# A layer of attention and experts on one core: first scores ahead of the last input projection, lists turned ahead of context products

## The reference

```python
def attn_projections(h, w_in, g_qa, g_ka):       # one projection, split into q, k, v of two head groups
    ...
    qa = rms_norm(heads(qa), g_qa)
    ka = rms_norm(heads(ka), g_ka)
    return qa, ka, heads(va), heads(qb), heads(kb), heads(vb)
...
def latent_layer(...):
    sh1, sc1, gt1, sh2, sc2, gt2 = modulation(c[:, None, :], w_ada, b_ada)
    h = modulate(x, g_pre_attn, sh1, sc1)
    qa, ka, va, qb, kb, vb = attn_projections(h, w_in, g_qa, g_ka)
    qa, ka = rope_2d(qa, rows, cols), rope_2d(ka, rows, cols)
    qb, kb = rope_2d(qb, rows, cols), rope_2d(kb, rows, cols)
    oa = blocked_gqa(qa, jnp.concatenate([k_a_ctx, ka], axis=1), jnp.concatenate([v_a_ctx, va], axis=1))
    ob = windowed_gqa_with_ctx(qb, kb, vb, k_b_ctx, v_b_ctx, sink_b)
    o = jnp.einsum('btk,kd->btd', jnp.concatenate([oa, ob], axis=-1), w_out)
    x = x + gt1 * rms_norm(o, g_post_attn)
    return ffn_sublayer(x, sh2, sc2, gt2, ...)
...
def expert_choice_moe(h, w_router, w_gate, w_up, w_down):
    cap = CAPACITY_FACTOR * T // N_EXPERTS       # 64 latent rows or 16 context rows for each of 16 experts
    aff = jax.nn.softmax(logits, axis=-1)
    g, idx = lax.top_k(jnp.swapaxes(aff, 1, 2), cap)
    xg = jax.vmap(lambda hb, ib: hb[ib])(h, idx)
    a = jnp.einsum('becd,edf->becf', xg, w_gate)
    u = jnp.einsum('becd,edf->becf', xg, w_up)
    y = jnp.einsum('becf,efd->becd', jax.nn.silu(a) * u, w_down) * g[..., None]
    # rows are added back at their tokens
```

## Time and profile before

| what | us |
|---|---|
| median of 3 runs | 955.2 (954.45 to 956.45) |
| the profiled execution | 957.28 |
| its span on the engines | 955.5 |
| PE busy in it | 899.5 (94%) |
| DVE busy | 361.2 (38%) |
| ACT busy | 216.5 (23%) |

### The profile page before, as it was taken

How to read it: one execution, slowest core, us unless ns; L and a number is a source line. 1 busy time by engine, 2 the same in 40 slices (tenths; PEclk the granted TensorE clock), 3 DMA queues, 4 the chain that set the end, 5 groups by cost and what they waited for, 6 DMA issues and landing times.

```text
span 955.5 us, 19886 instructions
## 1 busy us (share of the span) xinstructions
PE 899.5 (94%) x8653; PEld 444.0 (46%) x8653; DVE 361.2 (38%) x953; ACT 216.5 (23%) x526; POOL 89.2 (9%) x124
## 2 busy tenths in 40 slices
PE   3999998899899999779999999999999999999996
PEld 3544444777656565533344443444344334433442
DVE  4255635787767765811112031111111120310126
ACT  3132223676644653410000000000000000000002
POOL 2021200000000000100110111011101100110111
PEclk9999998899999999789999999999999999999998
DMA  9996532300000006959999999999999999999973
GB/s 337 347 373 264 221 132 99 116 2 1 2 1 23 23 23 226 414 185 371 398 395 412 398 398 398 409 397 397 408 399 398 396 410 399 397 400 392 340 277 139
DMA packets 76629, 265.58 MB, mean 278 GB/s; under 512 B 6032, under 2 KB 9808, under 8 KB 76544
## 3 DMA queue, kind: packets, MB, share of 16 engines
q1 hardware_dynamic: 71088, 248.53, 66.3%
q0 software_dynamic: 3792, 12.78, 4.8%
q10 hardware_dynamic: 1664, 3.01, 0.8%
HBM read 251.27 MB, written 13.04 MB: 277 GB/s over the span
## 4 chain that ended last, share of the span: by engine, by line
PE 70%; DMA 14%; SPq 5%; DVE 4%; ACT 3%; issue 2%; POOL 1%; ACTq 0%; POOLq 0%; DVEq 0%
PE ps L927 25%; PE ps L939 12%; DMA ring<-in_w_down 8%; PE ps L635 7%; PE ps L790 6%; SPq L467 5%; PE ps L611 4%; PE ps L741 3%; PE ps L719 3%; PE ps L706 2%; DMA reg_qt<-in_w_gate 2%; DMA ring<-in_w_ada 2%; PE ps L561 2%; ACT ring L1277 1%; DMA reg<-rows_l,kt 1%
## 5 line engine op out<-in xcount | busy, mean ns | idle before, releaser
L927 PE MATMUL ps<-ring,reg 128*32 128x512 f32 x1792 | 201.8, 592 | 0.0
L1809 DVE TENSOR_SCALAR mod<-ps,kt 64x512 f32<-64x512 f32 x30 | 22.5, 750 | 258.7 <-PE ps L927 258.5
L927 PEld LDWEIGHTS ps<-ring,reg 128*32 128x32 f32 x1792 | 58.1, 110 | 112.4 <-issue 103.8
L1329 ACT ACTIVATE reg<-ps 128x256 f32<-128x256 f32 x16 | 6.1, 384 | 386.3 <-PE ps L990 375.4
L939 PE MATMUL ps<-ring,values_in 128*32 128x256 f32 x1536 | 91.5, 380 | 1.5 <-DMA ring<-in_w_up 1.1
L927 PE MATMUL ps<-ring,kt 128*32 128x512 f32 x768 | 86.8, 592 | 0.0
L790 PE MATMUL ps<-ring,reg 128*128 128x512 f32 x160 | 76.4, 604 | 0.0
L939 PEld LDWEIGHTS ps<-ring,values_in 128*32 128x32 f32 x1536 | 48.7, 110 | 50.9 <-issue 16.4
L635 PE MATMUL ps<-ring,reg_qt 128*128 128x512 f32 x160 | 70.6, 594 | 0.0
L939 PE MATMUL ps<-ring,reg 128*32 128x256 f32 x1024 | 62.9, 388 | 3.0 <-DMA ring<-in_w_down 2.2
L1277 ACT ACTIVATE ring<-ps 128x640 f32<-128x640 f32 (+3 forms) x80 | 44.4, 555 | 73.3 <-PE ps L719 70.6
(11 more groups left out here) (224 smaller groups left out, 1001.2 us busy)
## 6 DMA issues: line engine op xcount, KB each, us to landing
ring<-in_w_up SPq DMA_DIRECT2D x32, 2048.0 KB, 24.4
ring<-in_w_down SPq DMA_DIRECT2D x32, 2048.0 KB, 24.6
ring<-in_w_gate SPq DMA_DIRECT2D x16, 2048.0 KB
reg_qt<-in_w_gate SPq DMA_DIRECT2D x16, 2048.0 KB
ring<-in_w_ada SPq DMA_DIRECT2D x12, 2048.0 KB, 11.7
reg<-in_x_sample SPq DMA_DIRECT2D x8, 512.0 KB, 6.6
ring<-in_w_in SPq DMA_DIRECT2D x2, 2048.0 KB, 17.0
ring<-in_w_out SPq DMA_DIRECT2D x2, 2048.0 KB, 10.0
```

The lines of the kernel that those rows point to most:

```text
L927: last = pe.matmul(o[64 * n + r:64 * n + r + 32, :], x(4 * hf + j, r), w[:, j, n * HALF:(n + 1) * HALF], start=(hf == 0 and j == 0), stop= ...
L1809: dve.tensor_scalar(put_l[:, n * HALF:(n + 1) * HALF], ps[rows, 3, :], g_l[rows, e:e + 1], None, ALU.mult)
```

## The change

Two passages are reordered. At the start of attention, `scores(0)` is issued before the last input projection, and the maxima and the exponential of unit 0 before what DVE and ACT do for that projection; the rotation of the last tile moves on DVE behind the weighting of unit 0, its low part behind that of unit 3, its turn on PE behind `scores(3)`. For this, banks are dealt out anew (`turned`, `scores_at`), and the stores of keys and values go from ACT's queue to SP's, behind the last output weight. Between attention and experts, the four casts of the second gate stand around `turn_x1(4)`, the last affinities are turned behind the first context rows, `turn_lists` comes ahead of the context products with the up weights, `turn_rows_l(0)` ahead of those with the down weights, and the context product with slot 7 moves into `gate_product(1, 1)`. Two fillers, `keep_busy`, multiply the identity by itself into unused columns. Lines of the diff that only move a function are left out.

```diff
@@ -257,7 +257,9 @@
 
         def turned(k):
 
-            return ps[:, (6 + k % 2) if k < 4 or k >= 3 * TILES - 1 else (5 if k % 2 else 2), :]
+            if k < 4 or k == 3 * TILES:
+                return ps[:, 6 + k % 2, :]
+            return ps[:, 5 if k % 2 else (2 if k < 2 * TILES else 6), :]
...
         def scores_at(u):
 
-            return two[u % 2] if u < A_UNITS else ps[:, u % 2, :]
+            return two[(u + 1) % 2] if u < A_UNITS else ps[:, (u + 1) % 2, :]
...
+            sp.wait_ge(rot_ready, 1)
+            for n, first in enumerate((0, P, 2 * P, 3 * P)):
+                sp.dma_start(out[2 + n][0, 0].rearrange("t h d -> t (h d)"), kv_ctx[:, first:first + P]).then_inc(stored, 16)
...
+            def scores(u):
+                g, h, t = HEAD_UNITS[u]
+                if u in (0, A_UNITS):
+                    pe.wait_ge(qkT_ready, (2 + g) * TILES + 1)
+                    pe.wait_ge(qkT_act, (2 + g) * TILES + 1)
+                if u == 1:
+                    pe.wait_ge(nat_ready, 3 * TILES)
+                if u >= 2:
+                    pe.wait_ge(exp_done, u - 1)
...
                     mod_columns(COLS[ADA_AFTER[i - 2]], ADA_AFTER[i - 2])
+                if i == 3 * TILES - 2:
+                    scores(0)
             turn_qk(3 * TILES - 1)
             spread_shift()
-
...
+            scores(1)
...
                 bank = 6 + k % 2 if k < A_UNITS // 2 else 7
-                if k == 0:
-                    pe.wait_ge(qkT_ready, 3 * TILES + 1)
-                    pe.wait_ge(qkT_act, 3 * TILES + 1)
+                if k < 2:
+                    pe.wait_ge(qkT_ready, 3 * TILES + k)
+                    pe.wait_ge(qkT_act, 3 * TILES + k)
                 if k >= 2:
...
-                    bank = 1 + 2 * (r % 2)
+                    bank = 4 * (r % 2)
                     if r == 0:
                         pe.wait_ge(gate_gained, 2)
-                        pe.wait_ge(h2_ready, 2 * TILES)
-                        pe.wait_ge(rows_c_ready, 3)
+                        pe.wait_ge(pT_ready, n_units)
+                        pe.wait_ge(logits_ready, TILES - 1)
                 if r >= 2:
...
-            scores(0)
-            scores(1)
-            turn_qk(3 * TILES)
             for u in range(n_units):
                 if u:
                     turn_probs(u - 1)
@@ -846,6 +847,8 @@
                     scores(u + 2)
                 if u % 2 and u >= 3:
                     values((u - 3) // 2)
+                if u == 1:
+                    turn_qk(3 * TILES)
...
+            def keep_busy(bank, n):
+
+                for _ in range(n):
+                    pe.matmul(ps[:, bank, 256:256 + P], ident[:, :], ident[:, :], start=True, stop=True)
+
+            for r in (0, 1):
+                cast_gate(1, r)
+            keep_busy(7, 6)
             turn_x1(4, 0)
             turn_x1(4, 1)
+            for r in (2, 3):
+                cast_gate(1, r)
             route_logits(4)
             turn_aff(3)
-            turn_aff(4)
...
             pe.wait_ge(logits_ready, TILES)
             turn_rows_c(0)
-            for r in (0, 1):
-                cast_gate(1, r)
+            turn_aff(4)
+            pe.wait_ge(gate_ready, 8)
...
-            for r in (2, 3):
-                cast_gate(1, r)
             turn_rows_c(1)
+            keep_busy(3, 4)
+            turn_lists()
             pe.wait_ge(silu_done, 1)
             weight_in(2, 0)
             product_c(2, GC[:, QUART:], context_of(0))
             weight_in(3, 0)
             product_c(3, GC[:, QUART:], context_of(0))
             gate_in(0, 0, 1)
-            product_c(SLOTS, GC[:, 0:QUART], context_of(1))
-            turn_lists()
-            gate_in(1, 0, 1)
-            product_c(SLOTS + 1, GC[:, 0:QUART], context_of(1)).then_inc(up_c, 1)
+            product_c(SLOTS, GC[:, 0:QUART], context_of(1)).then_inc(up_c, 1)
+            pe.wait_ge(xc_ready, 2)
+            turn_rows_l(0)
...
-            pe.wait_ge(xc_ready, 2)
-            turn_rows_l(0)
...
-            pe.wait_ge(gate_ready, 8)
             gate_l(0, 0)
...
             turn_rows_l(1)
-            gate_l(1, 1)
+            gate_product(1, 1)
...
+                if i == 3 * TILES - 2:
+                    exponentials(0)
             high_part(3 * TILES - 1)
...
-            act.wait_ge(rot_ready, 1)
-            for n, first in enumerate((0, P, 2 * P, 3 * P)):
-                act.dma_start(out[2 + n][0, 0].rearrange("t h d -> t (h d)"), kv_ctx[:, first:first + P]).then_inc(stored, 16)
...
-            exponentials(0)
             for u in range(n_units):
                 if u:
                     copy_pT(u - 1)
                 if u + 1 < n_units:
                     exponentials(u + 1)
-                if u == 0:
+                if u == 2:
                     high_part(3 * TILES)
                 o, j = divmod(u - A_UNITS, HEADS)
...
             exp_logits(3)
             square_half(1)
+            for r in (0, 1):
+                copy_gate(1, r)
             square_x1_half(0)
             square_x1_half(1)
             normalise_x1(4)
             store_rows(4)
+            for r in (2, 3):
+                copy_gate(1, r)
             exp_logits(4)
             def modulate_c(g):
 
                 act.wait_ge(xc_turned, g + 1)
...
+                act.wait_ge(stored, 16 * 4)
...
-            for i in range(3 * TILES):
+            for i in range(3 * TILES - 1):
...
+            maxima(0)
+            dve.wait_ge(shift_turned, 1)
+            dve.tensor_scalar(rb_col, ps[0:E, 7, 0:2], -1.0, None, ALU.mult).then_inc(shift_copied, 1)
+            low_part(3 * TILES - 2)
+            dve.wait_ge(consts_in, 16 * N_CONSTS)
+            link(dve.tensor_scalar(nsink[:, :], sink[:, :], -1.0, None, ALU.mult))
+
+            low_part(3 * TILES - 1)
+
+            def rotate_last():
+
+                i = 3 * TILES - 1
+                dve.wait_ge(nat_ready, i + 1)
+                dve.wait_ge(qk_turned, i)
+                dve.wait_ge(rot_ready, i)
+                rotate(rot[:, i % 2, :].rearrange("p (h d) -> p h d", d=DH), nat[:, i % 2, :], HEADS, rope, LT - 1)\
+                    .then_inc(rot_ready, 1)
+
...
                 if u == 0:
+                    rotate_last()
+                if u == 3:
                     low_part(3 * TILES)
...
```

72 lines of the change are left out of this document (24 added, 48 removed).

## The result

The changed kernel took 950.3 us (median of 7 runs, 947.27 to 952.15), the kernel before 954.6 beside it (7 runs, 953.34 to 957.07): ratio 0.9939, 95% interval 0.9924 to 0.9955, which is 5.8 us less (4.3 to 7.3). The ratio and its interval are taken over all runs; the two medians alone differ by 4.3 us, the lower end of it. The forecast was 949.9, range 946.8 to 953.2. The profiled execution of the change took 952.15 us for a span of 950.4, against 957.28 and 955.5.

The account below looks back on a forecast made before the run. The chain up to `gate_l(0, 0)`, then the weight stream, was taken to bound the kernel. Gains of 2.3 us at attention's start and 3.0 before the experts made 5.3, from 955.2 to 949.9 us, range 946.8 to 953.2.

Parts of the forecast that it names:

- What bounds the kernel: One chain up to `gate_l(0, 0)` sets the end; in the expert stage the weight stream is slightly slower than TensorE.
- The first place: Projections giving way to attention: unit 0 ahead of the last projection gains 2.3 us (1.4 to 3.3).
- the lead at full clock: Attention's start: unit 1's transposes come 3.0 us earlier, VectorE keeps pace to unit 4, so a lead of 2.9 us stands.
- Rival (c): Attention's start gives nothing, since rotation and low part only come later in VectorE's queue: 952.2 us; chance 0.10.
- The second place: Between attention and experts: earlier lists and gather start `gate_l(0, 0)` 3.0 us earlier (ends 1.1 and 5.4).
- The router's product: Between attention and experts: near 1.8 us as a sign of full clock from 384 to 393, against 3.56 at half clock.
- The second selection: Between attention and experts: starts 0.5 us after its 394.41 of before, ends 0 and 2.
- Rival (a): The latent rows' gather gets half the engines, taking 5.8 us, 2.5 less than the 8.3 used: 947.4 us; chance 0.12.
- The product over slot 7 behind `gate_l(0, 0)`: Expert stage: 1.93 us more TensorE work there fills waits of 2.2; costed at 0, with 1.9 as other end.
- rival (b): TensorE, not the weight stream, sets the expert stage, and 1.9 us comes back: 951.8 us; chance 0.15.
- Rival (d): Both passages at their low ends and TensorE setting the expert stage: 0.6 us gained, 954.6, no tellable change; chance 0.11.
- rival (e): Slower through the expert weight stream's rate: 1% less costs 4.4 us, at 2% the kernel takes 958.7; chance 0.06.

Follow-up runs that it names:

- the second place alone: The kernel before with only the passage between attention and experts reordered, attention's start left old: ratio 1.0003 (955.65 us), run again unchanged 0.9991 (954.5 us).
- the first place only: The changed kernel with everything from the last output projection on put back in the old order, fillers and casts included: 951.9 us, ratio 0.9962 to the kernel before.

## Why the prediction was right, point by point

**What bounds the kernel** held in every trace. The last column of the table, 527.5 to 528.3 us in twelve traces whose `gate_l(0, 0)` lies anywhere from 414.36 to 427.58, is the strongest evidence: whatever brought that product forward brought the end forward alike, and nothing done behind it counted. The restart of the stream is 3.7 us behind it (3.5 expected, 426.51 less 422.84).

**The first place: mechanism right, the term of 2.3 us too small.** It measured 3.6 (2.2 to 5.1) alone. This interval still takes in 2.3; the traces don't. TensorE's small products with the router's weights (L661 before, L666 in the change, at 149.79 and 150.10 in the first traces) stand ahead of all that was moved. From their start to the lists of context rows it takes 233.7 to 235.0 us in the four traces without the edit and 229.7 to 231.4 in the eight with it, means 234.2 and 230.3: 3.9 us. To unit 4's transposes it takes 29.3 and 25.8 in the mean, 3.6 us.

Unit 0's transposes came at 165.31 for 165.1, unit 4's at 176.17 for 176.5. The clock did fall, as said, and the transposes took 1.33. Even the price was right: in the three traces where unit 1's transposes ran at full clock (0.77 or 0.78), unit 4's came 25.5 us behind the mark, and 25.9 to 26.1 in the four where they took 1.33. So the half clock cost 0.4 to 0.6, where I had taken 0.6 (2.9 less 2.3). The failing step is the one before, the lead at full clock: "near 176 with the router's weights, against 178.8". With the 25.5 of full clock unit 4 stands at 175.3 on the clock of the earlier trace rows, against 179.10, a lead of 3.8 and not 2.9. VectorE's queue had summed to just these 175.3; the 0.7 that I laid on top for the router's weights never showed. Rival (c) falls with the run of this place alone, whose interval doesn't reach zero.

**The second place: the term of 3.0 us too large.** By the ratios it is worth 1.4 to 2.2 us on top of the first place (0.9962 less 0.9939 to 0.9947; by plain medians, each over that of the kernel before beside it, 0.7 to 0.9), and next to nothing alone. The intervals overlap, so the runs' times alone don't show a gain here. By the length in the traces it saves about 2: 41.1 us in the mean of the five executions that have it and none of the further edits (40.41 to 42.44, the one without filler among them) against 43.1 in the three that don't (41.28 to 44.07); the two sets overlap. In the first traces it was 4.74 less 3.1, 1.6. Step by step:

- The router's product took 1.85 at full clock, for 1.8. Right, but not by the filler. The full clock foretold from 384 to 393 held only to 389.
- The second selection started at 393.24. On the new clock (3.1 less) this is 2.0 late, at my upper end, where I had taken 0.5. The failing step is "The last affinities then stand behind eight turns of context rows (1.04)": I had counted the turns and not what they waited for, 2.25 us for a gather that landed 8.3 behind its issue. Behind this wait the turns ran at half clock, which is 0.9 us of the lateness. In other executions they didn't: the last affinities were turned 12.4 us behind the lists of context rows in the two traces where the turns took 1.94, and 10.9 to 11.3 in the five where they took 1.06 to 1.16.
- The lists were turned at 406.03 for 405.6, the gather issued 1.1 behind them for 0.8, and landed 8.2 later, inside the 7.6 to 9.0 of the earlier trace rows. In all seven traces in which slot 7's weights were queued beside it, it landed 7.4 to 8.5 behind its issue. Rival (a), half of the engines for the gather, is refuted: its 5.8 us would have had it at 412.9 and not 415.30. By the Trainium skill, page "DMA: Bandwidth & Descriptors", section "Queues, rings and completion order", the engines take turns between queues packet by packet; here that did not give a small gather its half of the bandwidth, though in the profile of the change the packets of the two queues are alike in size (12.78 MB in 3792 on the gathers' queue, 248.80 MB in 71664 on the weights'). Why is open, and no run shows whether the profile counts as packets what the page calls so. What helps is fewer bytes beside it: 5.1 us with slot 7's weights held back.
- `gate_l(0, 0)` started at 422.84 for 422.4. Part of this closeness is luck: the turns of latent rows took 1.94 for 1.04, the two products behind them 4.79 for 5.57.
- The product over slot 7 behind `gate_l(0, 0)` costs nothing there, as taken. The earlier trace rows had left out 1.1 us of waits for up weights, so that 3.3 us of waits were there to be filled, and 2.0 are left. The run with the product put ahead again shows it, and refutes rival (b). By that run the move carries the place's gain, 2.3 to 3.1 us by the ratios. I had named it only as a possible cost, while my 3.0 rested on it: in my sum no product with slot 7 stands between the gather and `gate_l(0, 0)`. What I had put on the early lists alone is what went missing.

The sum came out right, 5.3 us for 5.8 by the ratio (4.3 between the medians of the set), because the two errors point in opposite directions: 1.3 us too little at the first place, 0.8 to 1.6 too much at the second. That is luck. Part of the second error lies in the trace that I read: the second place of before was 44.06 long in the first execution and 41.28 in the next, with a clock that fell in one of them. I had scaled to the medians by 2.1 us for the whole, but had not asked which of the place's rows that excess sat in.

Rival (d) is excluded by the interval (0.9955 at the most), rival (e) by the slices, which show no slower stream.

**What stays open:** why the second place alone gives less (0 to 1 us) than on top of the first (1.4 to 2.2). The intervals allow the same 1 us for both. Executions of one kernel differ ahead of the place already (the change's lists at 380.40 and 378.78, of which 1.0 us arose before the router's weights at 150.10 and 149.08), and the clock fell in different places, so single traces can't settle it. Why the small gather doesn't get its share beside the weights is open too.

## What to carry to other kernels

Find the one instruction from which the way to the end has a constant length, and judge each edit by where that instruction starts; here one column of a table told more than any list of busy times. When work is pulled forward to issue a transfer early, look at what is in the DMA queues at the new time: the gather gained 7.4 us at its issue and TensorE kept 4.7, and holding back 2 MB, first used 24 us after their late issue, brought 3.8 to 4.6 us more, where the whole change had brought 5.8. And before costing a stall at half clock, compare two executions of the same kernel, since such a drop comes and goes, and see where each stands among its runs: here one was of an execution 2 us above the median of its runs, the other of one 2 us below.

## What the runs showed of the hardware

- A gather of 0.5 MB landed 7.4 to 8.5 us behind its issue in the seven traces with both gate halves of expert 1 queued beside it, 5.1 with one of them held back, and 4.5 in the emptying queue of the earlier trace rows.
- A stall of the same length did not have the same effect on the clock each time. Behind 2.87 us of idle TensorE, at the same place in the same order of instructions, the next two products took 2.46 and 3.64 us with the first place only, and 1.93 each in the second trace of the kernel before. In the two traces of the second place alone, 3.23 us were followed by turns of 1.06 (full clock) and 2.90 by turns of 1.94 (half).
- The clock also fell where the trace has TensorE busy throughout: 0.50 from 366 to 368 us in the second run of the second place alone.
- Without fillers the clock was 1.00 from 384 to 387 us beside the casts; ten filler products more changed nothing (0.9944 and 0.9947).
- One kernel's executions place the same product up to 3.5 us apart (`gate_l(0, 0)` of the change at 422.84 and 419.38), though their medians over a set of runs agree to 0.1%.
